# Gated attention's projections by seven half-size products per pair of tiles, with the gated results kept in memory

## What is computed

```python
# h: (1024 tokens, 1024); per head: q, k (1024, 128), v, g (1024, 256), log_a (1024, 128)
cum = cumsum of log_a inside chunks of 64
q_in, k_in = q * exp(cum), k * exp(-cum)
o_intra = tril(q_in k_in^T) v            # inside a chunk
S = S * exp(cum_last) + k_dec^T v        # from chunk to chunk, k_dec = k * exp(cum_last - cum)
y = rms_norm(o_intra + q_in S) * silu(g) # then y @ w_out is added to the residual
```

## Time and profile before

| | us |
|---|---|
| median of three runs (lowest, highest) | 2945.49 (2944.64, 2946.81) |
| span of the profiled execution | 2948.9 |
| TensorE busy | 2814.8, 95% |
| VectorE, ScalarE, GpSimd busy | 1718.4, 1063.7, 1342.8 |
| mean granted TensorE clock | 0.984 of full |
| GLA, from the gates of head 0 to the output projection | 1517.1 to 1866.3 |

### The profile page before, as it was taken

How to read it: one execution, slowest core, us unless ns; L and a number is a source line. 1 busy time by engine, 2 the same in 40 slices (tenths; PEclk the granted TensorE clock), 3 DMA queues, 4 the chain that set the end, 5 groups by cost and what they waited for, 6 DMA issues and landing times. The chain is left out here.

```text
span 2948.9 us, 39343 instructions
## 1 busy us (share of the span) xinstructions
PE 2814.8 (95%) x13278; PEld 2180.1 (74%) x13278; DVE 1718.4 (58%) x2188; ACT 1063.7 (36%) x1407; POOL 1342.8 (46%) x1652
## 2 busy tenths in 40 slices
PE   5999999998999999999989999999999999996997
PEld 3688888866877777787768888777677777774775
DVE  7679998988263612663563324263466666667453
ACT  5344444444120100000233232232466666665232
POOL 2344444447754433544723333577422222224775
PEclk9999999999999999999999999999999999998998
DMA  7522122155421132112331111333301000000423
GB/s 302 177 71 65 61 68 68 61 181 176 138 73 53 41 132 78 40 46 83 117 101 36 32 33 42 121 94 90 116 29 30 30 31 30 29 29 8 161 81 115
DMA packets 89451, 241.15 MB, mean 82 GB/s; under 512 B 6961, under 2 KB 20353, under 8 KB 88577
## 3 DMA queue, kind: packets, MB, share of 16 engines
q1 hardware_dynamic: 59648, 172.58, 18.6%
q10 hardware_dynamic: 29696, 67.16, 6.3%
HBM read 207.20 MB, written 32.51 MB: 81 GB/s over the span
## 5 line engine op out<-in xcount | busy, mean ns | idle before, releaser
L630 PE MATMUL ps<-t_h_hi,t_wh 128*128 128x512 f32 x2464 | 1004.7, 408 | 42.6 <-POOLq L542 15.8
L631 PE MATMUL ps<-t_h_lo,t_wh 128*128 128x512 f32 x2464 | 978.6, 397 | 0.0
L632 PE MATMUL ps<-t_h_hi,t_wl 128*128 128x512 f32 x2464 | 978.5, 397 | 0.0
L534 POOL CAST t_wh<-t_wst 128x1024 fp32r<-128x1024 f32 (+2 forms) x306 | 315.1, 1030 | 1432.3 <-PE ps L632 1317.7
L539 POOL TENSOR_TENSOR t_wl<-t_wst,t_wh 128x256 fp32r<-128x256 f32 (+2 forms) x1224 | 931.5, 792 | 24.5
L630 PEld LDWEIGHTS ps<-t_h_hi,t_wh 128*128 128x128 f32 x2464 | 465.5, 189 | 198.6 <-issue 51.7
L632 PEld LDWEIGHTS ps<-t_h_hi,t_wl 128*128 128x128 f32 x2464 | 465.8, 189 | 113.3
L631 PEld LDWEIGHTS ps<-t_h_lo,t_wh 128*128 128x128 f32 x2464 | 466.3, 189 | 110.4 <-issue 6.1
L2255 DVE SCALAR_TENSOR_TENSOR ps<-t_upad,t_vec,ps 128x1024 f32<-128x1024 f32 x224 | 275.5, 1286 | 7.1 <-DVE ps L2249 0.8
L630 PE MATMUL ps<-t_y_hi,t_wh 128*128 128x512 f32 x512 | 206.2, 403 | 10.2 <-POOLq L542 9.1
L631 PE MATMUL ps<-t_y_lo,t_wh 128*128 128x512 f32 x512 | 202.8, 396 | 0.0
(11 more groups left out here) (345 smaller groups left out, 3851.9 us busy)
## 6 DMA issues: line engine op xcount, KB each, us to landing
t_wst<-w_even_in SPq DMA_DIRECT2D x40, 512.0 KB, 3.5
t_wst<-w_ple SPq DMA_DIRECT2D x64, 320.0 KB, 2.8
t_wst<-w_even_out SPq DMA_DIRECT2D x32, 512.0 KB, 3.6
t_wst<-w_fox_in SPq DMA_DIRECT2D x32, 512.0 KB, 3.5
t_modw<-w_mod SPq DMA_DIRECT2D x6, 2048.0 KB, 16.2
t_xr<-x_d ACTq DMA_DIRECT2D x6, 2048.0 KB, 13.4
t_wst<-w_gla_in SPq DMA_DIRECT2D x24, 512.0 KB, 3.9
t_wst<-w_odd_in_a SPq DMA_DIRECT2D x16, 512.0 KB, 3.6
```

The lines of the kernel that those rows point to most:

```text
L534: pool.tensor_copy(wh[b][:, 0:w], wst[b][:, 0:w]).then_inc(S("w_high"), 1)
L630: pe.matmul(o, w1, x1, start=start and k == 0, stop=False)
L631: pe.matmul(o, w1, x2, start=False, stop=False)
L632: last = pe.matmul(o, w2, x1, start=False, stop=stop and k == kts - 1)
```

## The change

In GLA all projections but head 0's q, k and v are made pair by pair. A pair is two output tiles (q and k; the two of v; the two of g). With the weights cut in four blocks (tile x half of the 1024 inputs) and the activation in four (half of the inputs x half of the tokens), seven products of 4 x 3 = 12 matmuls each (Strassen's scheme, Winograd's form) take the place of eight. VectorE makes the sums of the weight blocks (`sums`) and, once, the sums of the activation blocks in head 0 (eight buffers `t_f`, `t_r`, which take the place of `y_hi` and `y_lo`); GpSimd splits the seven operands into a ring of four halves (`split_operand`); the products accumulate in three PSUM banks (`pair`), and ScalarE (`copied`, `plain`) and VectorE (`evacuated`) take out first product, sums and results between them. The temporary blocks lie in the second token half of `h_hi` and `h_lo`. Values now come out with channels on the partitions and TensorE transposes them (`turn_gla_values`). Gated results of heads 0 to 2 are stored to memory (`y_d`) by ScalarE's queue and loaded back by SyncE's after the last pair; ScalarE, GpSimd and VectorE then split them. The running sum is scanned in eight pieces of 128. In head 3 the gate pair stands ahead of the scores.

The core of the diff (buffers, semaphore names and lines that only move are left out):

```diff
-    ("w_gla_in", 4, [1024] * 6),
+    ("w_gla_in", 1, [1024] * 4),
+GLA_PAIRS = ["G0"] + [kind + str(i) for i in range(1, 4) for kind in ("QK", "V", "G")]
+    OPERANDS = ["a11", "a12", "s2", "s1", "s3", "s4", "a22"]
+    MOVING = ["b11", "b21", "t2", "t1", "t3", "b22", "t4"]
...
+        def load_pair(n):            # SyncE
+            for r in range(4):
+                    sp.wait_ge(S("s_ready"), again("s_ready", 7 * (n - 1) + (1, 2, 5, 7)[r]))
+                    sp.wait_ge(S("s_sum"), again("s_sum", 4 * n))
...
+        def split_operand(n):        # GpSimd
...
+                pool.wait_ge(S("s_used"), again("s_used", n - 3))
+            hi, lo = ring(wh, n), ring(wl, n)
+            pool.tensor_copy(hi, src).then_inc(S("s_high"), 1)
+            for z in range(2):
+                pool.tensor_tensor(lo[:, c], src[:, c], hi[:, c].bitcast(F32), ALU.subtract).then_inc(S("s_low"), 1)
...
+                split_tile(name, 0, 2, T, widths, 0)
+                whole_h(0, 0, t_f[0], 0)
+                split_tile(name, 0, 3, T, widths, 0)
+                whole_h(1, 0, t_f[1], 4)
+                for n in range(NPAIR):
+                    if n in (0, 3, 6):
+                        causal(n // 3)
+                    split_pair(n)
+                causal(3)
...
+        def pair(n, y, x, v, free=None, inside={}):      # TensorE
+            into = {"a11": y, "a12": x, "s2": y, "s1": v, "s3": y, "s4": v, "a22": y}
+            for q, name in enumerate(OPERANDS):
+                pe.wait_ge(S("s_ready"), again("s_ready", 7 * n + q + 1))
+                if name == "s2":
+                    pe.wait_ge(S("s_copied"), again("s_copied", 3 * n + 1))
+                if name == "s3":
+                    pe.wait_ge(S("s_copied"), again("s_copied", 3 * n + 2))
+                if name == "s4":
+                    pe.wait_ge(S("s_copied"), again("s_copied", 3 * n + 3))
+                if name == "a22":
+                    pe.wait_ge(S("s_out"), again("s_out", 3 * n + 2))
...
+        for i in range(1, 4):
+            gla_gates(i)
+            pair(3 * i - 2, 0, 1, 2, lambda: pe.wait_ge(S("g_go"), i + 1))
+            pair(3 * i - 1, 3, 4, 5, ...)
+            if i == 3:
+                pair(3 * i, 2, 0, 1, ...)
+            gla_scores(i)
+            turn_gla_values(i)
+            gla_turn_keys(i)
+            gla_chunks(i)
+            if i < 3:
+                gla_gate_pair(i)
+        for b in range(2):
+            gla_square_sum(3, b, 6 + b)
...
+        for i in range(1, 4):                            # ScalarE
+            gla_decay(i)
+            copied(qk, 0, 2, 0)
+            gla_growth(i)
+            store_gated(i - 1)
+            copied(qk, 0, 2, 1)
+            copied(qk, 0, 2, 2)
+            gla_shrink(i)
+            plain(qk, 0, kdt[:, 0:HALF])
+            copied(vv, 3, 5, 0)
+            gla_to_end(i)
...
+        for dst, c, k0 in ((2, 1, 4), (3, 0, 4)):        # VectorE, head 0, four 128x2048 sums more behind
+            line.go(TT_(t_f[dst][:, :].rearrange("p (k t) -> p k t", k=4), half3(h_hi, c, k0), half3(h_lo, c, k0), ALU.add))
...
+        sums(0)
+        mask_and_copy(0)
+        states(0)
...
+            if i < 3:
+                evacuated(gg, 0, 5, att[:, 0:HALF])
+                evacuated(gg, 1, 4, kdt[:, HALF:T])
+                sums(gg + 1)
+                evacuated(gg, 2, 6, att[:, HALF:T])
+            outs_scaled(i)
+        for v, y in enumerate((kdec, kin)):              # VectorE, after head 3
+            for c in range(2):
+                line(TT_(y[:, c * HALF:(c + 1) * HALF], y[:, c * HALF:(c + 1) * HALF], silu_g[v][c][:, :], ALU.mult))
+            line(dve.tensor_copy(col(y_hi, 6 + v), y[:, :]))
+            TT_(col(y_lo, 6 + v), y[:, :], col(y_hi, 6 + v).bitcast(F32), ALU.subtract).then_inc(S("g_y"), 1)
+        for k in (4, 5):
+            TT_(col(y_lo, k), col(y_lo, k).bitcast(F32), col(y_hi, k).bitcast(F32), ALU.subtract).then_inc(S("yg_rest"), 1)
```

More of the change, by code:

```diff
@@ L497, in _ @@
             for half in range(passes(name)):
+                if name == "w_gla_out" and half == 0:
+                    sp.wait_ge(S("s_ready"), again("s_ready", 7 * NPAIR))
+                    for j, w in enumerate(widths):
+                        load_tile(name, 0, j, sum(widths[:j]), w, widths)
+                    load_gated()
+                    with sp.Fori(0, times - 1) as i:
+                        for j, w in enumerate(widths):
+                            load_tile(name, i + 1, j, sum(widths[:j]), w, widths)
+                    continue
                 with sp.Fori(0, times) as i:
@@ L518, in split_tile @@
             b = wbuf(name, j)
[L519 to L528, removed]
             pool.wait_ge(S(f"w_loaded{b}"),
@@ L1077, in gla_head, with gla_square_sum @@
                         last.then_inc(S("g_o"), 1)
-            pe.wait_ge(S("g_st"), 16 * i + 16)
-            take(nm, i, 4)
-            project(wbuf(nm, 4), slot(2), h_hi, h_lo).then_inc(S("w_used"), 1)
+        def gla_square_sum(i, b, o):
             pe.wait_ge(S("g_sum"), i + 1)
-            for b in range(2):
-                last = pe.matmul(bank(6 + b), ones, osq[:, b * HALF:(b + 1) * HALF], start=True, stop=True)
-            last.then_inc(S("g_ss"), 1)
-            take(nm, i, 5)
-            pe.wait_ge(S("g_g0"), i + 1)
@@ L1088, in gla_head, with gla_gate_pair, sums @@
-            project(wbuf(nm, 5), slot(2), h_hi, h_lo).then_inc(S("w_used"), 1)
-        gla_head(0, begun=True)
-        with pe.Fori(0, 3) as i:
-            gla_head(i + 1)
-        pe.wait_ge(S("w_used"), first["w_gla_out"] + 2)
-        end(pe)
+            pe.matmul(bank(o), ones, osq[:, b * HALF:(b + 1) * HALF], start=True, stop=True).then_inc(S("g_ss"), 1)
+        def gla_gate_pair(i):
+            n = 3 * i
+            def sums():
+                gla_square_sum(i, 0, 7)
+                pe.wait_ge(S("s_out"), again("s_out", 3 * n + 1))
+                gla_square_sum(i, 1, 5)
+            pair(n, 4, 5, 6, lambda: pe.wait_ge(S("g_st"), 16 * i + 16), {2: sums})
@@ L2591, in gla_head, with to_chunk_end @@
-            dve.wait_ge(S("g_exp"), 4 * i + 4)
-            TT_(kdec[:, :], slot(1), kdec[:, :], ALU.mult).then_inc(S("g_kdec"), 1)
+            for n in range(8):
+                two = dve.tensor_tensor_scan(out=col(cum, n, 2 * CH), data0=cmask[:, :], data1=col(te, n, 2 * CH),
+                                             initial=0.0, op0=ALU.mult, op1=ALU.add)
+                if n < 7:
+                    line.go(two)
+            two.then_inc(S("g_cum"), 1)
+        def to_chunk_end(i):
+            TT_(c3(kdec), c3(cum)[:, :, CH - 1:CH].to_broadcast((P, 16, CH)), c3(cum), ALU.subtract).then_inc(S("g_cl"), 1)
@@ L2628, in _ @@
+        dve.wait_ge(S("g_y"), 8)
         end(dve)
```

430 lines of the change are left out of this document (366 added, 64 removed).

## The result

The changed kernel took 2977.3 us (median of 4 runs, 2976.5 to 2979.1), the kernel before beside it 2946.2 (2944.6 to 2949.6): ratio 1.0106, 95% interval 1.0093 to 1.0118. Forecast were 2968 and slower; it is slower, and by 9 us more than the likeliest value, inside the range.

The account below looks back on a forecast made before the run. TensorE alone was taken to bound the stage by heads. Head 0 +4.5, heads 1 and 2 -2.3 and the end +11.8 gave +14.0, with the clock +23 on the median 2945.5: 2968 us, range 2949 to 2981.

Parts of the forecast that it names:

- The work: TensorE in the stage by heads: ten pairs save 28.0 us, three heads' value transposes add 5.3, net -22.7 us.
- Head 0: First head, gates to next gates: VectorE's added sums delay the mask, partly offset elsewhere; +4.5 us, plus 0 to 3.4 of clock.
- The mask's wait: Before head 0's attention product: TensorE stands 7.4 us until GpSimd's mask, behind VectorE's sums; 5.4 net against before.
- the clock: Behind idle stretches TensorE runs at half clock for 3.4 to 6.8 us; cost taken as 9 of at most 14.6 us.
- The third: Before the next head's gates: VectorE's evacuations, sums and scalings end about 1.8 us after TensorE's products.
- The first: Third product of the QK pair, heads 1 to 3: TensorE stands 3.2 us for ScalarE's copy behind the decay chain.
- The second wait's chain: Before the fifth product: scans, exponential, two store issues and copy end at 17.5 against 16.4, a wait of 1.0 us.
- The end: Head 3 and first output tile: uncovered chain, output projection 11.3 us after the chunks, late low parts; +11.8 us, clock 0 to 4.
- The sum: Whole stage: 4.5 - 2.3 + 11.8 = +14.0 us, with the clock +23.
- The rivals: Hand-overs cost nothing, 2941 (chance 0.12); GpSimd becomes the bound, about 2990 (0.08); a wash, 2949 (0.08).
- the hand-overs cost nothing: Rival: waits between engines and the slow clock behind them vanish in three heads, 18 us less, giving 2941; chance 0.12.
- 12 from rows and 17 from the rule: GpSimd beside VectorE's two-input work: 12 or 17 us added to its 53 a head, both staying under the head's 88.

Follow-up runs that it names:

- experiment 7: Changed kernel with head 0's order, ScalarE's copies early, outputs scaled ahead of all four sums and the end reordered together: 2941.5 us, ratio 0.9988.
- experiment 6: Changed kernel with only the end reordered: y tiles copied and split before the squares, two output tiles started early: 2971.9 us, ratio 1.0086.
- experiment 11: Changed kernel with outputs scaled ahead of all four sums and the factor's logarithms ahead of ScalarE's fifth-product copy: 2969.0 us, ratio 1.0086.
- Experiment 10: Changed kernel with only 22 products without a use in head 0's wait before the attention product: 2973.7 us, ratio 1.0110.
- experiment 4: Changed kernel, order unchanged, with 85 products without a use in TensorE's waits: 2968.4 us, ratio 1.0076.
- experiment 3: Changed kernel with a head's outputs scaled after two of the next pair's four sums instead of behind all four: 2975.2 us, ratio 1.0102.
- experiment 5: Changed kernel with head 0's mask copy and first eight states ahead of the sums: 2974.3 us, ratio 1.0093.
- experiment 2: Changed kernel with ScalarE's copies in heads 1 to 3 moved ahead of the decay's logarithm and the growth: 2971.2 us, ratio 1.0084.
- experiment 8: As experiment 7, plus 16 products without a use where TensorE waits for the last head's outputs: 2942.6 us, ratio 0.9990.

## Why the forecast was right, and where it was off

**The work.** In heads at clock 1.00 with few waits (experiment 7) TensorE is busy 82.0 and 81.9 us, against 88.35: 6.4 us a head saved where three pairs less the transposes gave 6.6. Right.

**Head 0** was the step most mis-sized: +4.5 and at most 3.4 of clock forecast, +10.8 measured. The mask's wait was put at 7.4 and was 5.46 in this trace. That is no shorter chain: the masked products started 48.9 us after the gates here and 49.5 in two others (experiments 6 and 11), where TensorE had come at the full clock and stood 7.6 and 7.8. Here 3.4 us at 0.50 right after the gates made it later. The term that failed is the clock: not 3.4 to 6.8 us behind the wait but 13.70, with TensorE busy 11.87 of them, so 5.9 us lost. Experiment 10 gives back 5.0.

**Heads 1 to 3, the three waits.** Forecast 3.2, 1.0, 1.8 us; measured 1.02, 0.20, 1.05 at the third product, 1.64, 1.91, 1.63 at the fifth, and 2.84 (2.4 was said for head 0), 1.89, 1.89 at the gates. The third is right to 0.1 where it was forecast by itself. The first is right in its chain and was masked: wait for wait, TensorE went through gates and two products at half clock behind the gates' wait and so met the copy later. Where that clock is full (experiments 4 and 11) the wait is 2.6. The step that was off is the clock's place: it was put behind the first wait, and it stood behind the gates' wait, ahead of the first. The sum, 88.3 and 0.7 to 2.4 of clock, holds head 2 (90.61) and misses head 1 (91.25) by 0.6. Mended alone, head 0, copies, hand-over and end give 3, 6, 8 and 5 us by the medians (4, 6, 6 and 6 by the ratios), 22 in sum, and 36 together. Our reading is that a wait removed in one place leaves TensorE early for the next, as experiments 3, 5 and 11 show at single places; but each of these differences is uncertain by 3 to 5 us, and in experiment 7 the first copy stands earlier than in 2, so the surplus itself is not shown.

**The second wait's chain** was right in sum and wrong in its terms. The copy for the fifth product was to end 17.5 us after the gates; in head 3, with the least slow clock, it ends at 17.7. But the eight scans, put at 3.1 us (bounds 2.3 and 4), took 4.93, 5.36 and 4.93 in heads 1 to 3 and 7.46 in head 0; and the two store issues, put at 1.06 on top of the exponential, ran beside it, so that the misses nearly cancel: luck. In experiment 4 GpSimd has nothing to do for 5.0 us at that place, and the same eight scans take 2.63. So the added time goes with GpSimd's work beside them, and it stands in the chain that ends the second wait.

```profile
1797.70 4.93 DVE L2932 TENSOR_TENSOR_SCAN t_cum<-t_cmask,t_te 128x128 f32<-128x128 f32 x8
1802.67 1.06 ACT L1993 ACTIVATE t_te<-t_cum 128x1024 f32<-128x1024 f32 x1 [4.62 <-DVE t_cum L2932]
1802.67 0.33 ACTq L2024 DMA_DIRECT2D y_d<-t_kdec  x1
```

Experiment 4, the same scans, and GpSimd's next instruction with its idle time:

```profile
1609.59 2.63 DVE L2942 TENSOR_TENSOR_SCAN t_cum<-t_cmask,t_te 128x128 f32<-128x128 f32 x8
1613.48 0.61 POOL L661 CAST t_wh<-t_wst 128x512 fp32r<-128x512 f32 x1 [5.01 <-PE ps L1221]
```

**The end.** 3.65 and the rest to 11.3 us before the output projection, 3 to 5 at its fifth row: measured 3.50, 5.77 and 3.20, each ended by what was named; the output projection starts 13.0 us after the chunks and not 11.3, with the ones-matmuls at half clock in between. (The forecast's terms for the gates of head 3 to the end of the first tile add up to 108.6 and not to the 108.9 that it took.) From gates to the end of four output tiles it is +15.3 against +11.8 and clock; the 17.1 us at 0.50 hold only 9.27 of TensorE's work, 4.6 lost.

**The stores.** They were said to end before the next write of kdec. They didn't: ScalarE stood 3.1 us for them in head 2, beside TensorE's work and at no cost.

```profile
1718.21 1.06 ACT L1998 ACTIVATE t_kdec<-t_cum 128x1024 f32<-128x1024 f32 x1 [3.11 <-DMA y_d<-t_kin]
```

**The sum.** The stage was forecast at +23 and came to +29.0: 2.9 of the 6 are head 0's beyond its upper bound, the rest is the clock of heads 1 to 3 and the end taken near the middle of bounds of which the upper ends came. The other 3 of the 9 us are not placed: the traced executions differ by 26.1 us and the medians by 31.2. The runs of the changed kernels take 2.1 to 2.4 us more than their spans; if that holds for the traced execution of before, it took some 5.6 us more than its median, and not 3.4. The clock was put at 9 us in all, and filling the waits gave back 9. That agreement is partly luck: the filled kernel still has clock 0.96 to 0.98 in three of its four parts, since the slow stretches moved, in heads 1 to 3 behind the first wait. What the clock costs in full stays open.

**The rivals.** That the hand-overs cost nothing is refuted by experiments 2 and 11. GpSimd never ended a wait of TensorE inside a pair; it ended the mask's, and it lengthened the scans behind the second. By its rows a head's 21 operands of 2.02 (0.61 and 1.41) and the mask would take 43.8 us alone; it was busy 51.70 in head 1. The 7.9 us more are from running beside VectorE, where one operand's subtractions took 5.42:

```profile
1586.29 0.61 POOL L661 CAST t_wh<-t_piece 128x512 fp32r<-128x512 f32 x1 [0.42 <-PE ps L1221]
1586.99 5.42 POOL L665 TENSOR_TENSOR t_wl<-t_piece,t_wh 128x256 fp32r<-128x256 f32 x2
```

The forecast had set 12 from rows and 17 from the rule of the Trainium skill (SBUF — State Buffer, Who interferes with whom). Here the loss on GpSimd is 7.9. Both figures took all of VectorE's two-input work to fall beside GpSimd's and all of the loss to fall on GpSimd. That either side can be held up, as that section says (issue order decides who blocks), the trace bears out: VectorE's sums of 0.69 took 0.99 to 1.22 beside GpSimd, and its scans nearly twice their time.

## What to carry to other kernels

When fewer products are bought with more steps between engines, list for each in-order queue what stands ahead of each release, for the product and for everything else the same engine owes the one that bounds; that list, and not the work saved, decided here: the same matmuls in another order are 36 to 40 us apart. Judge such a reordering with all hand-overs mended at once, since what one alone wins is in part given back at the next, and read the stretch beside the time. An idle TensorE costs again in the clock, so cover the longest waits first.

## What was not expected of the hardware

A wait of 1.89 us at the gates was followed by 6.8 us at 0.50 clock in head 2 and 3.4 in head 3, one of 5.46 by 13.7, one of 1.74 by 10.2. Before head 0's attention a wait of 1.43 us was followed by 10.2 us at 0.50 in experiment 5 and by none in 7 and 8; behind the waits of 1.1 to 1.4 us for the keys the clock stayed 1.00 in each. The half-clock stretches are thus not in proportion to the wait, and the two longest of the changed kernel lie over work of small or few matmuls: the attention products behind the mask (13.7) and the ones-matmuls of the end with their waits (17.1). In two traces (the changed kernel's and experiment 2's) 3.4 us at 0.50 stood behind head 0's gates, where TensorE had waited 0.2 us, and in the others none. And slowing down hides waits: at half clock the first wait of head 2 was 0.20 us and at the full one 2.6. Eight scans of 128x128 on VectorE took 2.63 us with GpSimd idle and 4.93 to 5.36 beside it.
